# The gated chunk mixer of a two-layer block: its group stages reordered, and its input weights kept as a bf16 copy in DRAM

## Chip, cores and metric

The kernel runs on all 8 cores of one Trainium2 chip. Each core computes one of the eight batch elements; the cores exchange nothing. The time is device microseconds of the slowest core.

## What is computed

Two layers over a sequence of 2048 tokens plus 256 context tokens, with 1024 features. Layer 0 mixes tokens by a gated MLP over chunks of 128 tokens, layer 1 by window attention; each is followed by a mixture of 16 experts that every token passes through densely. The change touches only the mixer of layer 0:

```python
def chunk_gmlp(h, w_in, g_v, w_s, b_s, w_out):      # h: normalized, modulated x
    uv = jax.nn.gelu(h @ w_in)                      # w_in 1024 x 4096
    u, v = jnp.split(uv, 2, axis=-1)                # 2048 + 2048 features
    v = rmsnorm(v, g_v).reshape(bsz, n // CHUNK, CHUNK, A_GROUPS, A_GW)
    v = jnp.einsum('gpq,bcqgd->bcpgd', w_s, v) + b_s.T[None, None, :, :, None]
    return (u * v.reshape(bsz, n, A_WIDTH)) @ w_out
...
x = x + g1 * chunk_gmlp(h, ...)                     # then the experts, attention, experts
```

## The kernel before

The program is a list of operations per engine, each in the order in which it is written. `Prog.op` gives every operation its waits from the buffers that it reads and writes; an engine takes its list strictly in order, and so do the two queues that issue transfers: POOL (all transfers that cast float32 to bf16) and SP (all others). A transfer that must wait holds up everything behind it in its queue. Phases follow one another with a barrier: modulation vectors, mixer (`phase_gmlp`), experts, attention, experts, final norm.

In `phase_gmlp` the 18 token tiles of 128 are taken in five groups, four of 4 tiles and a last one of 2. All 18 tiles of x live in SBUF in float32 (`C.x_sb`). Each group goes through four stages, one group after the other:

- **A**: SP loads the x tiles of the group (L576; 512 KB each; no buffer is reused, so nothing holds these loads back). `norm_stats` (L429 to L436) clears a sum on DVE, squares each tile on ACT with an accumulated sum, takes the square root on ACT and the reciprocal on DVE. Then for each tile DVE scales it (L448), TensorE transposes eight blocks (L475) into one PSUM bank, and ACT (L482, even tiles) or DVE (L486, odd tiles) writes the modulated result to `hTg`, of which there is one buffer.
- **B**: for four column pieces of w_in (1024 x 512, read as float32 from DRAM, 2 MB, and cast to 1 MB of bf16 in flight) POOL issues the load into one of two `wi` buffers (L585). TensorE does 32 matmuls on each (L593), and ACT applies gelu to give `uT`.
- **C**: the four pieces of the v half likewise (L601, matmuls L608, gelu to `vraw`); then the squares of v for its norm on ACT (L619), their sum (L622), root (L624) and reciprocal (L626).
- **D**: for each tile DVE scales v (L631), TensorE mixes the chunk (32 small matmuls, L639 and L642), DVE multiplies by `uT` (L645), TensorE multiplies by w_out (32 matmuls, L652), and DVE scales by the gate (L655) and adds to x (L658).

So the order on every engine is A, B, C, D of group 0, then A of group 1, and so on, and every group loads all eight pieces of w_in again: 40 loads on the POOL queue. With two `wi` buffers, piece p+2 can be loaded only once the matmuls of piece p are done. At the start of the phase POOL issues the small constants, then the two halves of w_out (L561), which wait for each other because they are noted as writes of one buffer, and then pieces 0 and 1; SP issues two gate vectors and all x tiles.

Of the kernel before, what the change touches and what calls it, by code (L numbers as in the profile page):

```python
# [6 lines left out]
BF16 = mybir.dt.bfloat16  # L7
# [233 lines left out]
def build_program(stop_after=None, dbg=False):  # L241
# [94 lines left out]
    if stop_after == "A":  # L336
        return finish(C)
    phase_gmlp(C)
    if stop_after == "B":
        return finish(C)  # L340
# [166 lines left out]
def phase_gmlp(C):  # L507
    nc, P, I = C.nc, C.P, C.I
# [3 lines left out]
    wi = [R.t("wi%d" % i, [128, 8, 512], BF16) for i in range(2)]  # L512
    wiB = P.bufs("wi", 2)
# [46 lines left out]
    for h in range(2):  # L560
        P.op("pool", lambda e, h=h: e.dma_start(out=w_out[:, h * 8:(h + 1) * 8, :],  # L561
                                               in_=I.a_w_out[h * 1024:(h + 1) * 1024, :].rearrange("(c p) f -> p c f", p=128)),
             writes=[woB], dma=True)

    groups = [[0, 1, 2, 3], [4, 5, 6, 7], [8, 9, 10, 11], [12, 13, 14, 15], [16, 17]]
    ring = [1, 2, 3]
    rk = 0
    pmk = 0
    wk = 0
    tk = 0  # L570
    for g in groups:
        n = len(g)
        N = 128 * n
        for i, t in enumerate(g):
            src = I.ctx[t * 128:(t + 1) * 128, :] if t < 2 else I.x[(t - 2) * 128:(t - 1) * 128, :]
            P.op("sp", lambda e, t=t, src=src: e.dma_start(out=C.x_sb[:, t, :], in_=src), writes=[C.xB[t]], dma=True)  # L576
        norm_stats(C, g, ssall, ssBt, rstd, rstdB, [sts[0]["xn"], sts[1]["xn"]], [sts[0]["xnB"], sts[1]["xnB"]], eps, epsB)
        for i, t in enumerate(g):
            who = 1 if t < 2 else 0
            norm_transpose_tile(C, R, C.x_sb[:, t, :], C.xB[t], layer, 0, who, hTg, hTgB, i * 128, sts, 0,  # L580
                                rstd_ap=rstd[:, i:i + 1], rstdB=rstdB)
        for jj in range(4):
            s = wk % 2
            wk += 1
            P.op("pool", lambda e, jj=jj, s=s: e.dma_start(  # L585
                out=wi[s][:], in_=I.a_w_in[jj].rearrange("(c p) f -> p c f", p=128)),
                writes=[wiB[s]], dma=True)
            for j4 in range(4):
                j = jj * 4 + j4
                pb = ring[rk % 3]  # L590
                rk += 1
                for k in range(8):
                    P.op("pe", lambda e, s=s, j4=j4, k=k, pb=pb, N=N: e.matmul(  # L593
                        C.ps[pb][:, 0:N], wi[s][:, k, j4 * 128:(j4 + 1) * 128], hTg[:, k, 0:N], start=(k == 0), stop=(k == 7)),
                        reads=[wiB[s], hTgB], writes=[C.psB[pb]])
                P.op("act", lambda e, j=j, pb=pb, N=N: e.activation(out=uT[:, j, 0:N], in_=C.ps[pb][:, 0:N], func=AF.Gelu_apprx_tanh),
                     reads=[C.psB[pb]], writes=[uTB])
        for sv in range(4):
            s = wk % 2
            wk += 1  # L600
            P.op("pool", lambda e, sv=sv, s=s: e.dma_start(  # L601
                out=wi[s][:], in_=I.a_w_in[4 + sv].rearrange("(c p) f -> p c f", p=128)),
                writes=[wiB[s]], dma=True)
            for i, t in enumerate(g):
                pb = ring[rk % 3]
                rk += 1
                for k in range(8):
                    P.op("pe", lambda e, s=s, k=k, pb=pb, i=i: e.matmul(  # L608
                        C.ps[pb][:, :], hTg[:, k, i * 128:(i + 1) * 128], wi[s][:, k, :], start=(k == 0), stop=(k == 7)),
                        reads=[wiB[s], hTgB], writes=[C.psB[pb]])  # L610
                P.op("act", lambda e, sv=sv, pb=pb, i=i: e.activation(out=vraw4[:, i, sv * 512:(sv + 1) * 512], in_=C.ps[pb][:, :],
                                                                      func=AF.Gelu_apprx_tanh),
                     reads=[C.psB[pb]], writes=[vrawB4[i]])
        for i in range(n):
            P.op("dve", lambda e, i=i: e.memset(ssv[:, i, :], 0.0), writes=[ssvBt[i]])
        for i in range(n):
            for hf in range(2):
                jb = sts[(2 * i + hf) % 2]
                P.op("act", lambda e, i=i, hf=hf, jb=jb: e.activation(out=jb["xn"][:, 0:1024], in_=vraw4[:, i, hf * 1024:(hf + 1) * 1024],  # L619
                                                                    func=AF.Square, accum_out=ssv[:, i, hf:hf + 1]),  # L620
                     reads=[vrawB4[i], ssvBt[i]], writes=[ssvBt[i], jb["xnB"]])
        P.op("dve", lambda e, n=n: e.tensor_tensor(out=rstdv[:, 0:n], in0=ssv[:, 0:n, 0], in1=ssv[:, 0:n, 1], op=ALU.add),  # L622
             reads=list(ssvBt[:n]), writes=[rstdvB])
        P.op("act", lambda e, n=n: e.activation(out=rstdv[:, 0:n], in_=rstdv[:, 0:n], func=AF.Sqrt, scale=1.0 / 2048, bias=eps[:, 0:1]),  # L624
             reads=[rstdvB, epsB], writes=[rstdvB])
        P.op("dve", lambda e, n=n: e.reciprocal(out=rstdv[:, 0:n], in_=rstdv[:, 0:n]), reads=[rstdvB], writes=[rstdvB])  # L626
        for i, t in enumerate(g):
            who = 1 if t < 2 else 0
            pp = tk % 2
            tk += 1  # L630
            P.op("dve", lambda e, i=i: e.scalar_tensor_tensor(out=vraw4[:, i, :], in0=vraw4[:, i, :], scalar=rstdv[:, i:i + 1], in1=gv[:],  # L631
                                                             op0=ALU.mult, op1=ALU.mult),
                 reads=[vrawB4[i], rstdvB, gvB], writes=[vrawB4[i]])
            for b4 in range(4):
                pm = 4 + (pmk % 2)
                pmk += 1
                for jq in range(4):
                    j = b4 * 4 + jq
                    P.op("pe", lambda e, pm=pm, jq=jq, j=j, i=i: e.matmul(  # L639
                        C.ps[pm][:, jq * 128:(jq + 1) * 128], vraw4[:, i, j * 128:(j + 1) * 128], wsT[:, j // 2, :], start=True, stop=False),  # L640
                        reads=[vrawB4[i], wsB], writes=[C.psB[pm]])
                    P.op("pe", lambda e, pm=pm, jq=jq, j=j: e.matmul(  # L642
                        C.ps[pm][:, jq * 128:(jq + 1) * 128], ones1[0:1, :], bsrow[0:1, j // 2, :], start=False, stop=True),
                        reads=[bsB], writes=[C.psB[pm]])
                P.op("dve", lambda e, pm=pm, b4=b4, i=i, pp=pp: e.tensor_tensor(  # L645
                    out=prodT[pp][:, 4 * b4:4 * b4 + 4, :], in0=C.ps[pm][:, :].rearrange("p (a n) -> p a n", a=4),
                    in1=uT[:, 4 * b4:4 * b4 + 4, i * 128:(i + 1) * 128], op=ALU.mult),
                    reads=[C.psB[pm], uTB], writes=[prodB[pp]])
            for half in range(2):
                pb = 6 + half  # L650
                for j in range(16):
                    P.op("pe", lambda e, pb=pb, j=j, half=half, pp=pp: e.matmul(  # L652
                        C.ps[pb][:, :], prodT[pp][:, j, :], w_out[:, j, half * 512:(half + 1) * 512], start=(j == 0), stop=(j == 15)),
                        reads=[prodB[pp], woB], writes=[C.psB[pb]])
                P.op("dve", lambda e, pb=pb, half=half, who=who, pp=pp: e.tensor_tensor(  # L655
                    out=tmpf[pp][:, half * 512:(half + 1) * 512], in0=C.ps[pb][:, :], in1=C.gbc[:, who, half * 512:(half + 1) * 512], op=ALU.mult),
                    reads=[C.psB[pb], C.gbcB[who]], writes=[tmpfB[pp]])
            P.op("dve", lambda e, t=t, pp=pp: e.tensor_tensor(out=C.x_sb[:, t, :], in0=C.x_sb[:, t, :], in1=tmpf[pp][:], op=ALU.add),  # L658
                 reads=[tmpfB[pp], C.xB[t]], writes=[C.xB[t]])


def _const_tables():
# [526 lines left out]
```

How the kernel before makes its waits and increments, by code:

```python
        def run(ename, eng):  # L152
            waited = {}
            for o in self.ops[ename]:
                need = {}
                for d in o.deps:
                    if d.sem is None:
                        continue
                    key = d.sem
                    if need.get(key, (0,))[0] < d.cnt:
                        need[key] = (d.cnt, d.sem)
                for key, (cnt, sem) in need.items():
                    if waited.get(key, 0) >= cnt:
                        continue
                    eng.wait_ge(sem, cnt)
                    waited[key] = cnt
                inst = o.fn(eng)
                if o.dma:
                    inst.then_inc(o.sem, 16)
                elif o.need_inc:
                    inst.then_inc(o.sem, 1)
```

## Time and profile before

| | us |
|---|---|
| median of 2 runs | 5187.08 (5054.29 and 5319.87) |
| profiled execution | 5052.77 |
| its span, slowest core (core 0) | 5051.2 |
| spans of the eight cores | 5020.7 to 5051.2 |
| TensorE matmuls busy in the span | 3964.6 (78%) |
| PE idle in the mixer until a w_in load landed | 53.1 + 49.9 |

The mixer with its first loads takes the stretch from about 230 to 1214 us of the span. The rows further down are of core 0, the slowest. A row of the timeline gives the start, the length, the engine and line, what is written from what, how many instructions were merged, and in brackets the idle time before it with what ended that. A row of the windows gives for a stretch the busy time and the number of instructions of each engine, then the granted TensorE clock as a share of 2.4 GHz, the share in which the 16 DMA engines were busy, and GB/s written.

### The profile page before, as it was taken

To read this page: it belongs to the slowest core of one execution; us is meant where nothing else is said; L and a number is where in the kernel's file an instruction comes from. 1 tells how busy PE (TensorE), PEld (TensorE's weight loads), DVE (VectorE), ACT (ScalarE), POOL (GpSimd) and SP (SyncE) were. 2 spreads that over 40 slices of the span, in tenths; PEclk is the share of its full clock that TensorE was granted. 3 is DMA by queue.
4 is the path that set the end of the run, shared out by engine and by line. 5 is a ranking of instruction groups with operands and counts; after the bars stand their busy time and mean duration, and the time that the engine had idled before them with its cause. 6 is when DMAs were issued, how large, how long until landed. Compare 5 with 4: busy or idle time off the path is not lost.

```text
span 5051.2 us, 56891 instructions; the slowest of 8 cores (5020.7 to 5051.2 us)
## 1 busy us (share of the span) xinstructions
PE 3964.6 (78%) x19632; PEld 1843.6 (36%) x19632; DVE 1704.1 (34%) x2756; ACT 928.8 (18%) x1703; POOL 1509.0 (30%) x897
## 2 busy tenths in 40 slices
PE   3255667564599999999999566666399999999994
PEld 0022222231244454454444332332244444444442
DVE  0002122122344444444443453111344444444444
ACT  0021211313211111111111323444311111111112
POOL 1000000000044444444454301222044444444442
PEclk7576777776699999999999798888599999999997
DMA  9681422415012113113111021000212121212111
GB/s 142 92 157 17 67 32 35 67 25 84 1 26 42 34 26 51 26 26 51 26 26 26 26 20 25 1 1 8 47 26 45 31 46 30 47 29 47 30 26 71
DMA packets 191273, 206.31 MB, mean 41 GB/s; under 512 B 33544, under 2 KB 165768, under 8 KB 190728
## 3 DMA queue, kind: packets, MB, share of 16 engines
q0 software_dynamic: 167424, 178.63, 23.4%
q1 hardware_dynamic: 23568, 24.03, 1.6%
q8 instruction: 164, 2.69, 0.2%
q14 instruction: 117, 0.96, 0.1%
HBM read 372.78 MB, written 8.49 MB: 75 GB/s over the span
## 4 chain that ended last, share of the span: by engine, by line
PE 71%; DMA 9%; DVE 6%; ACT 6%; issue 5%; POOL 4%; DVEq 0%; ACTq 0%; POOLq 0%; SPq 0%
PE ps L875 19%; PE ps L871 19%; PE ps L893 15%; DMA pb_wi<-a_w_in 4%; PE ps L652 3%; POOL x_sb L901 3%; DMA pa_wa<-ada_w 2%; PE ps L593 2%; PE ps L608 2%; PE ps L1050 2%; PE ps L1159 2%; PE ps L1131 2%; DVE hT L486 1%; ACT hT L482 1%; PE ps L639 1%
## 5 line engine op out<-in xcount | busy, mean ns | idle before, releaser
L901 POOL TENSOR_TENSOR x_sb<-x_sb,pc_tmpf 128x1024 f32<-128x1024 f32 x544 | 1260.9, 2352 | 1746.7 <-DVE pc_tmpf L897 1746.7
L871 PE MATMUL ps<-hT,pc_wg 128*128 128x512 bf16 (+1 forms) x4608 | 1037.2, 368 | 0.0
L875 PE MATMUL ps<-hT,pc_wu 128*128 128x512 bf16 (+1 forms) x4608 | 1034.3, 367 | 1.7 <-DVE pc_A L880 1.7
L893 PE MATMUL ps<-pc_wd,pc_A 128*128 128x512 bf16 x4352 | 964.3, 379 | 13.9 <-DVE pc_tmpf L897 13.9
L897 DVE SCALAR_TENSOR_TENSOR pc_tmpf<-ps,sm_gatesv,gbc 128x512 f32<-128x512 f32 x1088 | 815.9, 750 | 342.0 <-POOL x_sb L901 160.0
L880 DVE TENSOR_TENSOR pc_A<-ps,pc_sg 128x512 bf16<-128x512 f32 x576 | 380.9, 661 | 1293.7 <-PE ps L871 835.4
L878 ACT ACTIVATE pc_sg<-ps 128x512 bf16<-128x512 f32 x576 | 330.4, 574 | 2478.4 <-PE ps L871 2169.1
L871 PEld LDWEIGHTS ps<-hT,pc_wg 128*128 128x128 bf16 x4608 | 451.4, 98 | 493.9 <-issue 3.3
L875 PEld LDWEIGHTS ps<-hT,pc_wu 128*128 128x128 bf16 x4608 | 450.8, 98 | 492.2 <-issue 4.2
L893 PEld LDWEIGHTS ps<-pc_wd,pc_A 128*128 128x128 bf16 x4352 | 417.3, 98 | 539.2 <-issue 59.0
L585 POOL DMA_DIRECT2D pb_wi<-a_w_in x20 | 17.6, 879 | 665.1 <-PE ps L593 592.9
L1167 ACT ACTIVATE pd_PT<-ps 128x512 bf16<-128x512 f32 x312 | 162.4, 604 | 216.2 <-PE ps L1159 211.9
L593 PE MATMUL ps<-pb_hTg,pb_wi 128*128 128x512 bf16 (+1 forms) x640 | 147.0, 398 | 69.7 <-DMA pb_wi<-a_w_in 53.1
L639 PE MATMUL ps<-pb_wsT,pb_vraw 128*128 128x128 bf16 x288 | 81.5, 283 | 128.9 <-DVE pb_vraw L631 128.9
L608 PE MATMUL ps<-pb_wi,pb_hTg 128*128 128x512 bf16 x576 | 141.8, 409 | 50.0 <-DMA pb_wi<-a_w_in 49.9
L652 PE MATMUL ps<-pb_wout,pb_prodT 128*128 128x512 bf16 x576 | 162.8, 452 | 18.3 <-DVE pb_prodT L645 18.3
L390 PE MATMUL ps<-pa_wa,pa_sclhs 128*2 128x512 bf16 x192 | 78.2, 583 | 124.7 <-DMA pa_wa<-ada_w 90.1
L1159 PE MATMUL ps<-pd3b_qz,pd_kT 128*128 128x512 bf16 x312 | 103.7, 436 | 80.0 <-POOL pd3b_qz L1155 80.0
L622 DVE TENSOR_TENSOR pb_rstdv<-pb_ssv 128x4 f32<-128x4 f32 (+1 forms) x5 | 0.8, 162 | 433.6 <-ACT pb_xn L619 433.6
L475 PE MATMUL ps<-sm_ident_b,pb_xn 128*128 128x128 bf16 x144 | 18.2, 307 | 149.6 <-DVE pb_xn L448 107.2
L432 ACT ACTIVATE pb_xn<-x_sb 128x1024 bf16<-128x1024 f32 x18 | 18.8, 1047 | 594.6 <-DVE pb_ssall L429 348.9
L1172 PE MATMUL ps<-pd_v,pd_PT 128*128 128x65 bf16 x1248 | 86.7, 200 | 51.1 <-ACT pd_PT L1167 49.7
(149 smaller groups left out, 2134.2 us busy)
## 6 DMA issues: line engine op xcount, KB each, us to landing
pb_wi<-a_w_in POOLq DMA_DIRECT2D x40, 1024.0 KB, 10.3
pc_wg<-moe_w_gate POOLq DMA_DIRECT2D x32, 1024.0 KB, 9.5
pc_wu<-moe_w_up POOLq DMA_DIRECT2D x32, 1024.0 KB, 13.8
pc_wd<-moe_w_down POOLq DMA_DIRECT2D x32, 1024.0 KB, 18.1
pa_wa<-ada_w POOLq DMA_DIRECT2D x24, 1024.0 KB, 16.0
x_sb<-x SPq DMA_DIRECT2D x16, 512.0 KB, 29.8
out<-pf_ob SPq DMA_DIRECT2D x16, 512.0 KB, 2.6
pb_wout<-a_w_out POOLq DMA_DIRECT2D x2, 2048.0 KB, 34.0
```

The lines of the kernel that those rows point to most:

```text
L593: P.op("pe", lambda e, s=s, j4=j4, k=k, pb=pb, N=N: e.matmul(C.ps[pb][:, 0:N], wi[s][:, k, j4 * 128:(j4 + 1) * 128], hTg[:, k, 0:N], start ...
L608: P.op("pe", lambda e, s=s, k=k, pb=pb, i=i: e.matmul(C.ps[pb][:, :], hTg[:, k, i * 128:(i + 1) * 128], wi[s][:, k, :], start=(k == 0), st ...
L652: P.op("pe", lambda e, pb=pb, j=j, half=half, pp=pp: e.matmul(C.ps[pb][:, :], prodT[pp][:, j, :], w_out[:, j, half * 512:(half + 1) * 512] ...
L871: P.op("pe", lambda en, k=k, f=f, pg=pg: en.matmul(C.ps[pg][:, 0:N], Wg[s][:, k, f * 128:(f + 1) * 128], C.hT[:, k, tok0:tok0 + N], start= ...
L875: P.op("pe", lambda en, k=k, f=f, pu=pu: en.matmul(C.ps[pu][:, 0:N], Wu[s][:, k, f * 128:(f + 1) * 128], C.hT[:, k, tok0:tok0 + N], start= ...
L878: P.op("act", lambda en, q=q, pg=pg: en.activation(out=sg[q][:, 0:N], in_=C.ps[pg][:, 0:N], func=AF.Silu), reads=[C.psB[pg]], writes=[sgB[q]])
L880: P.op("dve", lambda en, f=f, q=q, pu=pu: en.tensor_tensor(out=A[:, f, tok0:tok0 + N], in0=C.ps[pu][:, 0:N], in1=sg[q][:, 0:N], op=ALU.mul ...
L893: P.op("pe", lambda en, f=f, half=half, pb=pb, t=t: en.matmul(C.ps[pb][:, :], A[:, f, t * 128:(t + 1) * 128], Wd[s][:, f, half * 512:(half ...
L897: P.op("dve", lambda en, half=half, pb=pb, t=t, who=who, q=q: en.scalar_tensor_tensor(out=tmpf[q][:, half * 512:(half + 1) * 512], in0=C.p ...
L901: P.op("pool", lambda en, t=t, q=q: en.tensor_tensor(out=C.x_sb[:, t, :], in0=C.x_sb[:, t, :], in1=tmpf[q][:], op=ALU.add), reads=[tmpfB[q ...
L1159: P.op("pe", lambda e, bi=bi, kc=kc, hk=hk, pq=pq, mi=mi: e.matmul(C.ps[bi][:, :], kT[:, hk, kc:kc + 128], qz[pq][:].rearrange("p a b -> p ...
L1167: P.op("act", lambda e, bi=bi, pq=pq: e.activation(out=PT[pq][:, bi, :], in_=C.ps[bi][:, :], func=AF.Exp, scale=0.125), reads=[C.psB[bi]], ...
```

## The change

Stage A becomes a function of its own, stages B and C another, D a third. They are issued as A(0), then for every group BC(g), A(g+1), D(g). So the norm and the transposes of the next group stand, on every engine and queue, ahead of stage D of this group. The x loads of a group are in its stage A, on the SP queue.

The pieces of w_in are loaded by `load_piece`. In group 0 each is loaded as before on the POOL queue, and SP then stores the bf16 tile to a new DRAM tensor `wsc`, with 8 KB contiguous for each partition. In groups 1 to 4 SP loads the piece from `wsc`, and POOL issues nothing. The store reads the `wi` buffer, so piece p+2 of group 0 waits for it too.

```diff
--- before.py
+++ after.py
@@ -568,7 +568,21 @@
     pmk = 0
     wk = 0
     tk = 0
-    for g in groups:
+    st8 = {"rk": 0, "pmk": 0, "wk": 0, "tk": 0}
+    wsc = nc.dram_tensor("w_in_bf16", [8, 128, 8 * 512], BF16, kind="Internal").ap()
+    wscB = P.bufs("wsc", 8)
+
+    def load_piece(pc, s, gi):
+        if gi == 0:
+            P.op("pool", lambda e: e.dma_start(out=wi[s][:], in_=I.a_w_in[pc].rearrange("(c p) f -> p c f", p=128)),
+                 writes=[wiB[s]], dma=True)
+            P.op("sp", lambda e: e.dma_start(out=wsc[pc], in_=wi[s][:].rearrange("p c f -> p (c f)")),
+                 reads=[wiB[s]], writes=[wscB[pc]], dma=True)
+        else:
+            P.op("sp", lambda e: e.dma_start(out=wi[s][:].rearrange("p c f -> p (c f)"), in_=wsc[pc]),
+                 reads=[wscB[pc]], writes=[wiB[s]], dma=True)
+
+    def stage_a(g):
         n = len(g)
         N = 128 * n
         for i, t in enumerate(g):
@@ -579,12 +593,15 @@
             who = 1 if t < 2 else 0
             norm_transpose_tile(C, R, C.x_sb[:, t, :], C.xB[t], layer, 0, who, hTg, hTgB, i * 128, sts, 0,
                                 rstd_ap=rstd[:, i:i + 1], rstdB=rstdB)
+
+    def stage_bc(g, gi):
+        n = len(g)
+        N = 128 * n
+        rk, wk = st8["rk"], st8["wk"]
         for jj in range(4):
             s = wk % 2
             wk += 1
-            P.op("pool", lambda e, jj=jj, s=s: e.dma_start(
-                out=wi[s][:], in_=I.a_w_in[jj].rearrange("(c p) f -> p c f", p=128)),
-                writes=[wiB[s]], dma=True)
+            load_piece(jj, s, gi)
             for j4 in range(4):
                 j = jj * 4 + j4
                 pb = ring[rk % 3]
@@ -598,9 +615,7 @@
         for sv in range(4):
             s = wk % 2
             wk += 1
-            P.op("pool", lambda e, sv=sv, s=s: e.dma_start(
-                out=wi[s][:], in_=I.a_w_in[4 + sv].rearrange("(c p) f -> p c f", p=128)),
-                writes=[wiB[s]], dma=True)
+            load_piece(4 + sv, s, gi)
             for i, t in enumerate(g):
                 pb = ring[rk % 3]
                 rk += 1
@@ -624,6 +639,11 @@
         P.op("act", lambda e, n=n: e.activation(out=rstdv[:, 0:n], in_=rstdv[:, 0:n], func=AF.Sqrt, scale=1.0 / 2048, bias=eps[:, 0:1]),
              reads=[rstdvB, epsB], writes=[rstdvB])
         P.op("dve", lambda e, n=n: e.reciprocal(out=rstdv[:, 0:n], in_=rstdv[:, 0:n]), reads=[rstdvB], writes=[rstdvB])
+        st8["rk"], st8["wk"] = rk, wk
+
+    def stage_d(g):
+        n = len(g)
+        pmk, tk = st8["pmk"], st8["tk"]
         for i, t in enumerate(g):
             who = 1 if t < 2 else 0
             pp = tk % 2
@@ -657,6 +677,16 @@
                     reads=[C.psB[pb], C.gbcB[who]], writes=[tmpfB[pp]])
             P.op("dve", lambda e, t=t, pp=pp: e.tensor_tensor(out=C.x_sb[:, t, :], in0=C.x_sb[:, t, :], in1=tmpf[pp][:], op=ALU.add),
                  reads=[tmpfB[pp], C.xB[t]], writes=[C.xB[t]])
+
+
+        st8["pmk"], st8["tk"] = pmk, tk
+
+    stage_a(groups[0])
+    for gi, g in enumerate(groups):
+        stage_bc(g, gi)
+        if gi + 1 < len(groups):
+            stage_a(groups[gi + 1])
+        stage_d(g)
 
 
 def _const_tables():
```

## Rows read from the trace of the kernel before

**Rows 1.** Windows by stage of core 0: busy us (and count) per engine, clock, DMA share, GB/s.

```profile
core 0: us, PE busy (x) PEld busy (x) DVE busy (x) ACT busy (x) POOL busy (x), PEclk, DMA share, GB/s
...
230.00:306.00 76.00, 4.05 (x32) 3.10 (x32) 8.98 (x30) 13.50 (x26) 4.72 (x6) 0.50 1.02 222
306.20:383.30 77.10, 64.14 (x256) 26.72 (x256) 0.00 (x0) 19.80 (x32) 6.12 (x7) 0.88 0.69 97
383.30:398.10 14.80, 0.00 (x0) 0.01 (x1) 2.69 (x3) 10.93 (x19) 0.87 (x1) 0.58 0.70 109
398.10:479.70 81.60, 63.67 (x256) 26.82 (x256) 26.37 (x29) 0.00 (x0) 0.00 (x0) 0.70 0.00 0
479.70:510.00 30.30, 4.05 (x32) 3.10 (x32) 10.38 (x31) 11.89 (x25) 0.00 (x0) 0.58 0.00 0
510.10:586.00 75.90, 61.05 (x256) 25.68 (x256) 0.00 (x0) 19.80 (x32) 6.11 (x7) 0.92 0.68 97
714.10:786.60 72.50, 62.20 (x256) 26.11 (x256) 0.00 (x0) 19.80 (x32) 6.12 (x7) 0.91 0.68 97
913.20:989.60 76.40, 64.42 (x256) 26.49 (x256) 0.00 (x0) 19.79 (x32) 6.11 (x7) 0.88 0.68 96
1103.30:1166.00 62.70, 36.88 (x192) 21.10 (x192) 0.00 (x0) 11.61 (x24) 5.25 (x6) 0.76 0.73 101
```

**Rows 2.** Waits of PE between 300 and 1240 us: total us, times, longest.

```profile
PE ps L593 <- DMA pb_wi<-a_w_in: 53.1, 6, 27.4
PE ps L608 <- DMA pb_wi<-a_w_in: 49.9, 17, 9.0
```

**Rows 3.** Timeline of PE, the first pieces of group 0.

```profile
306.22 16.14 PE L593 MATMUL ps<-pb_hTg,pb_wi 128*128 128x512 bf16 x64 [27.43 <-DMA pb_wi<-a_w_in]
327.39 15.66 PE L593 MATMUL ps<-pb_hTg,pb_wi 128*128 128x512 bf16 x64 [5.03 <-DMA pb_wi<-a_w_in]
```

**Rows 4.** Timeline of POOL, the loads of pieces 2 and 3 of group 0.

```profile
316.01 0.87 POOL L585 DMA_DIRECT2D pb_wi<-a_w_in  x1 [41.76 <-PE ps L593]
322.90 0.87 POOL L585 DMA_DIRECT2D pb_wi<-a_w_in  x1 [6.02 <-PE ps L593]
```

**Rows 5.** Transfers issued, from the page: count, KB each, median us to landing.

```profile
pb_wi<-a_w_in POOLq DMA_DIRECT2D x40, 1024.0 KB, 10.3
...
x_sb<-x SPq DMA_DIRECT2D x16, 512.0 KB, 29.8
out<-pf_ob SPq DMA_DIRECT2D x16, 512.0 KB, 2.6
```

**Rows 6.** Timeline of the SP queue in the attention phase, two 1 MB loads.

```profile
2841.67 0.33 SPq L985 DMA_DIRECT2D pd_cosT<-rope  x1
2846.66 0.33 SPq L986 DMA_DIRECT2D pd_sinT<-rope  x1
```

**Rows 7.** Waits of the SP queue around those loads.

```profile
SPq L165 <- DMA pd_sinT<-rope: 6.2, 1, 6.2
SPq L165 <- DMA pd_cosT<-rope: 4.6, 1, 4.6
```

**Rows 8.** Windows with dense matmuls in the expert phase.

```profile
2000.00:2100.00 100.00, 100.00 (x496) 48.26 (x495) 41.06 (x58) 12.28 (x22) 48.05 (x25) 1.00 0.24 36
```

**Rows 9.** Windows at the start of the phase, and while a piece is loaded alone.

```profile
260.00:272.00 12.00, 2.02 (x16) 1.55 (x16) 4.88 (x12) 3.66 (x8) 0.66 (x1) 0.50 1.04 278
...
321.00:333.00 12.00, 6.97 (x26) 2.62 (x24) 0.00 (x0) 1.74 (x4) 0.87 (x1) 0.86 1.11 162
```

**Rows 10.** Tile of w_out until 310 us: its two loads and their landing times.

```profile
L561 POOL DMA_DIRECT2D pb_wout<-a_w_out x2: 926/1000/1073, 231.3 to 271.3; - x2
...
DMA to landing us min/median/max: 28.5/34.0/39.4
```

**Rows 11.** Tile of wi until 312 us: landing times of pieces 0 and 1.

```profile
DMA to landing us min/median/max: 33.6/35.6/37.7
```

**Rows 12.** Timeline between stage C and stage D of group 0.

```profile
395.23 0.18 DVE L626 RECIPROCAL pb_rstdv<-pb_rstdv 128x4 f32<-128x4 f32 x1 [1.84 <-ACT pb_rstdv L624]
```

**Rows 13.** Timeline of stage A of group 1, between D(0) and B(1).

```profile
481.99 1.06 ACT L432 ACTIVATE pb_xn<-x_sb 128x1024 bf16<-128x1024 f32 x1 [86.93 <-DVE pb_ssall L429]
...
487.93 1.01 PE L475 MATMUL ps<-sm_ident_b,pb_xn 128*128 128x128 bf16 x8 [8.26 <-DVE pb_xn L448]
...
507.77 2.14 DVE L486 TENSOR_SCALAR pb_hTg<-ps,sm_cols 128x128 bf16<-128x128 bf16 x5 [0.46 <-DVE pb_hTg L486]
```

## Prediction

> **What bounds the kernel now.** I read the windows by stage first. Outside the mixer nothing is touched, so the question is how much of the stretch from 230 to 1214 us is not matmul at full speed. In the expert phase TensorE is busy all of a 100 us window at a granted clock of 1.00, that is 2.4 GHz [rows 8]. In the mixer the stages with eight weight pieces (B and C, "BC" below) take 77.1, 75.9, 72.5, 76.4 and 62.7 us [rows 1]. What they would take without waiting comes from the POOL queue: it issues a load when a buffer comes free, and the buffers of pieces 0 and 1 came free at 316.01 and 322.90 [rows 4]. So 32 matmuls of 512 columns take 6.9 us at 2.4 GHz (0.215 us each), and eight pieces 55.2 us. BC of a full group is 17 to 22 us longer.
>
> Where these go is in the waits and in TensorE's timeline: pieces go in pairs, 64 matmuls and then some 3 to 5 us until a w_in load lands [rows 2, 3]. The pause costs twice. The first pair after it takes 15.66 us where 13.8 would do [rows 3]: after idling, the engine runs at 1.2 GHz before it is granted 2.4 again, hence a mean clock of 0.88 to 0.92 in BC [rows 1]. The load is the limit: issued at 316.01, its piece's matmuls begin at 327.39, 11.4 us later, of which 10.3 us is landing [rows 3, 4, 5]. One buffer's load (11.4) and the other buffer's piece (6.9 and up) don't fit in two pieces of matmuls (13.8). Three further stretches matter: 76 us of loads ahead of the first piece [rows 1], 14.8 us between C and D and 30.3 us between D and the next B [rows 1].
>
> **Term 1, the pieces of groups 1 to 3.** A load from the copy is 1 MB without a cast, 8 KB for each partition. The trace has that very transfer: the cosine table, 1 MB of 128 rows of 8 KB, issued on SP in 0.33 us, kept the queue waiting 4.6 us until it landed; the next one, which shared the engines with two other transfers, 6.2 us [rows 6, 7]. I take 5.0 us from a free buffer to data, bounds 4.9 and 11.4 (as now). As 5.0 is under 6.9, no piece waits. BC is then 55.2 us, plus 0.4 for the last matmul's end and 0.4 for a slow start: 56.0. Today B starts after transposes at a clock of 0.50 to 0.58 [rows 1]; after the change it comes straight behind D's dense matmuls. Gains: 75.9, 72.5 and 76.4 less 56.0 each, together 56.8.
>
> A rule of the Trainium skill speaks against this: the page "TensorE: Matmul & The Clock Gate", Part 1, says that a die goes to 13/16 of the clock once three of its cores run dense matmuls. This case's trace disagrees, for all eight cores run the expert phase and the slowest core is granted 1.00 there [rows 8]. By the page BC would be 68 us instead of 56.
>
> **Term 2, group 4.** Two tiles, so a piece is half as long, 3.45 us, and now the load of 5.0 doesn't fit: a pair of pieces takes 5.4 + 3.45 = 8.9 us (0.4 for waking both engines). Three such pairs and a last pair of 6.9 are 33.6 us; with 1.5 us at the low clock 35. Today 62.7: gain 27.7. Bounds: 20 if the pauses keep the clock at 0.76, as there now [rows 1], and 29.
>
> **Term 3, the start.** Today 18 x tiles (9 MB) share the DMA engines with w_out: 278 GB/s in all [rows 9], and the two halves of w_out, one behind the other, land 39.4 and 28.5 us after issue at 231.3 and 271.3 [rows 10]. Pieces 0 and 1 are issued at 272.4 and land 33.6 and 37.7 us later, at 306.0 and 311 [rows 11]. In the new order SP issues only four x tiles before it meets the first store, and the other 14 tiles (7.2 MB) go elsewhere. Data up to the first half's landing: gate vectors 1 MB, x 2 MB, constants 0.8, half of w_out 2 = 5.8 MB at the stretch's mean of 222 GB/s [rows 1] from 230 on: 256, and some us later for a start slower than the mean: 259. The second half: a lone cast load of 1 MB lands in 10.3 us [rows 5], of which the bytes take 6.2 at 162 GB/s [rows 9], so 4 us go before and after; 2 MB at 278 GB/s are 7.5 us, at 200 they are 10: 272. Piece 0 follows directly with 6.2 us and the same 4: 282. hTg is ready about then too: TensorE's last transposes ended 27.4 us before 306.2 [rows 3], at 279, and their evacuation takes 3 or 4. With both ends so near each other I take B(0) to start at 286, a gain of 20. Bounds: 5, if the other traffic only filled gaps, and 24.
>
> **Term 4, the stores of group 0.** Eight stores of 1 MB on SP, each behind the landing of its piece. A 512 KB store lands in 2.6 us [rows 5]; for 1 MB I take 4.5. It starts with the piece's matmuls (6.9 us), so the buffer is not held longer. But it shares the DMA engines with the cast load of the next piece, and group 0 is still bound by those loads. Moving it takes 2.7 us at most of another load's time. Half of the stores fall into the 5 us between an issue and its first bytes: four that cost up to 2.7, less what the idle pause absorbs: 6 us lost, bounds 0 and 20. The page "DMA: Bandwidth & Descriptors", Anatomy of one DMA, warns that the receipt of a write can be surprisingly long when the target is HBM; the 2.6 us of the output stores don't show it. Were a store 10 us long, each pair would lose some 5, in all the 20 of the bound.
>
> **Term 5, the boundaries.** Stage A(g+1) moves in front of D(g). Today, from the end of C to D is 14.8 us and from the end of D to B 30.3, together 45.1 [rows 1]. New: the reciprocal of v's norm ends at 395.4, 12.1 after C's end [rows 12]; the squares of x can start then. From the first square to the last evacuation today is 481.99 to 509.9, 27.9 us [rows 13]. Then comes DVE's scaling of v with 2.6 us (395.4 to 398.1 [rows 12, 1]) and D begins: 12.1 + 27.9 + 2.6 = 42.6. After D, TensorE goes straight on with B. Gain 2.4 per boundary, four of them: 9, bounds 0 and 14. So the reordering hides almost nothing: the work of A sits in front of D on ACT, DVE and TensorE alike, and D waits in its place; what is hidden is only the tail of D on DVE (L655, L658).
>
> **What else moves.** Of stage A four more operations change their queue position: the x loads. In SP they stand behind store 7 of group 0, which waits for the landing of piece 7, some 7 us before C ends. Four tiles (2 MB at 222 GB/s, 9.5 us, plus the store) land about 6 us after C's end, and ACT asks for the first at 12.1: hidden by 6 us. In later groups they stand behind the load of piece 7, issued when piece 5 is done, 14 us before C's end: hidden. Pieces 0 and 1 of the next group stand behind them but have the 82 us of D [rows 1]. Lines on POOL vanish; nothing waited for POOL but these loads.
>
> **Sum.** -56.8 - 27.7 - 20 + 6 - 9 = -107.5 against the profiled 5052.77 us (its span is 5051.2), so 4945; I write 4947, as a core with shorter pauses today, and so less to gain, may then be the last. The other run shown is 5319.87 and the median 5187; the sum is against the lower of the two, with which the profiled execution agrees.
>
> **Rivals.**
> (a) **The loads are slower than the table's**, because eight cores read at once for long: landing 8 us instead of 4.6. For it: sinT's 6.2. Against it: cosT was read by all cores too. Each pair of pieces then waits about 1.5 us and gets the slow start of 1.9 again: 3 pauses of 3.4 us in 3 groups, and 13 us in group 4 (4 pairs, 3.2 each), together 44 less gain: 4991.
> (b) **The clock is held at 13/16 in BC.** 12 us more in four groups, less what group 0 hides: about 44 (36, and 8 in group 4): 4991. Against it [rows 8].
> (c) **The x loads become the wait.** If they land in 29.8 us, as the median now [rows 5], instead of about 13, issued 7 us before C ends: 23 after, 11 later than ACT asks, in group 0, and 4 in the others: 20 us: 4967. Against it: now 18 are in flight together.
> (d) **Slower than before.** The mechanism is the piece load from the copy alone: if it takes longer than the cast, all of groups 1 to 4 pay. Terms 3 to 5 give 23 us; each us of landing over today's 10.3 costs 3 per full group and 4 in the last, 13; it decides above 12 us. At the 29.8 us of the x loads, 19.5 x 13 - 23 = 230 more: 5283. Only [rows 5] speaks for it, and [rows 6, 7] against.
> (e) **The copy isn't what the loads take**, or they aren't shortened: only terms 3 to 5: 5030.
>
> **Chances.** Forecast 0.70, with its own range 4922 to 4972; (a) 0.10, (b) 0.05, (c) 0.07, (d) 0.03, (e) 0.05. 2% is about what a measurement can tell here, and it lies at 4952, inside the forecast's range: some 0.66 of the forecast's 0.70 falls below, and none of the others. So faster 0.47, within 2% 0.50, slower 0.03. The range holds the forecast, (a), (b) and (c): 4915 to 5000.
>
> **What would show it.** Right: no wait for a w_in load in BC of groups 1 to 3, BC of 56 us at a clock near 1.00; landing near 5 us on SP; the first piece at about 286; C to D about 43 us, D to B none. Wrong: pauses between pieces, a wait for x in stage A, BC(0) over 90 us, or D no longer 82 us.

## The result

The changed kernel is faster, by about 2%: the ratio of its runs to those of the kernel before is 0.9804, 95% interval 0.9753 to 0.9855. So it is clear that it is faster, and not whether by more than 2%. Its profiled execution took 4951.95 us against 5052.77, and was forecast at 4947. Some executions of either kernel had a lower TensorE clock on one die or both and are left out of the comparison (all but one of 4999.34 us; the other six in it took 4942.14 to 4951.95), and they are why the plain medians (4999.34 of 11 runs, 5309.07 of 10 before) are higher.

### The profile page after: what moved, and what is told of

Same layout as the page of the kernel before. It is cut to its first block, busy times and chain, and to the rows that moved or that the text cites. A ratio compares the mean times of both kernels' runs of the same rounds, so it can differ in the third digit from the quotient of the medians.

```text
span 4950.3 us, 56912 instructions; the slowest of 8 cores (4935.4 to 4950.3 us)
## 1 busy us (share of the span) xinstructions
PE 3945.8 (80%) x19632; PEld 1842.4 (37%) x19632; DVE 1703.9 (34%) x2756; ACT 928.6 (19%) x1703; POOL 1481.2 (30%) x865
## 4 chain that ended last, share of the span: by engine, by line
PE 73%; DMA 6%; DVE 6%; ACT 6%; issue 5%; POOL 4%; DVEq 0%; ACTq 0%; POOLq 0%; SPq 0%
PE ps L905 19%; PE ps L901 19%; PE ps L923 15%; PE ps L672 3%; POOL x_sb L931 3%; DMA pa_wa<-ada_w 2%; PE ps L623 2%; PE ps L610 2%; PE ps L1189 2%; PE ps L1080 2%; PE ps L1161 2%; DVE hT L486 1%; ACT hT L482 1%; DMA pb_wi<-a_w_in 1%; PE ps L659 1%
## 5 line engine op out<-in xcount | busy, mean ns | idle before, releaser
L610 PE MATMUL ps<-pb_hTg,pb_wi 128*128 128x512 bf16 (+1 forms) x640 | 132.8, 371 | 16.5 <-DMA pb_wi<-a_w_in 13.6
L623 PE MATMUL ps<-pb_wi,pb_hTg 128*128 128x512 bf16 x576 | 130.6, 388 | 18.1 <-DMA pb_wi<-a_w_in 13.6
L839 PE MATMUL ps<-pc_wr,hT 128*128 128x16 bf16 x272 | 12.3, 174 | 142.1 <-ACT hT L482 77.8
L482 ACT ACTIVATE hT<-ps,sm_cols 128x128 bf16<-128x128 bf16 x208 | 95.2, 458 | 145.8 <-PE ps L475 128.5
## 6 DMA issues: line engine op xcount, KB each, us to landing
pb_wi<-a_w_in POOLq DMA_DIRECT2D x8, 1024.0 KB, 13.9
```

The lines of the kernel that those rows point to most:

```text
L610: P.op("pe", lambda e, s=s, j4=j4, k=k, pb=pb, N=N: e.matmul(C.ps[pb][:, 0:N], wi[s][:, k, j4 * 128:(j4 + 1) * 128], hTg[:, k, 0:N], start ...
L623: P.op("pe", lambda e, s=s, k=k, pb=pb, i=i: e.matmul(C.ps[pb][:, :], hTg[:, k, i * 128:(i + 1) * 128], wi[s][:, k, :], start=(k == 0), st ...
```

## The profile after

The windows by stage of the changed kernel, core 6, its slowest (columns as in [rows 1]): BC of group 0, C to D, D, BC of group 1, C to D, D, and BC of groups 2, 3 and 4.

```profile
287.90:371.80 83.90, 66.14 (x256) 26.81 (x256) 0.00 (x0) 19.80 (x32) 5.26 (x6) 0.82 0.92 193
371.80:414.20 42.40, 4.12 (x34) 3.17 (x33) 11.04 (x28) 22.80 (x44) 0.00 (x0) 0.54 0.25 82
414.20:496.40 82.20, 64.33 (x256) 27.05 (x257) 26.38 (x29) 0.00 (x0) 0.00 (x0) 0.68 0.00 1
496.40:551.90 55.50, 55.46 (x257) 24.95 (x255) 1.96 (x6) 19.79 (x32) 0.00 (x0) 1.00 0.48 163
551.90:594.20 42.30, 4.23 (x33) 3.20 (x33) 11.05 (x28) 22.80 (x44) 0.00 (x0) 0.55 0.11 35
594.20:676.40 82.20, 64.33 (x256) 27.05 (x256) 26.37 (x29) 0.00 (x0) 0.00 (x0) 0.69 0.00 1
676.40:732.40 56.00, 55.58 (x257) 24.90 (x255) 1.95 (x6) 19.80 (x32) 0.00 (x0) 1.00 0.48 164
857.40:912.70 55.30, 55.30 (x258) 24.95 (x255) 1.95 (x6) 19.80 (x32) 0.00 (x0) 1.00 0.42 152
1024.50:1061.80 37.30, 30.33 (x193) 18.94 (x191) 1.94 (x4) 11.61 (x24) 0.00 (x0) 0.95 0.47 170
```

Against [rows 1], BC of groups 1 to 3 fell from 75.9, 72.5 and 76.4 us to 55.5, 56.0 and 55.3, with TensorE busy throughout and the clock up from about 0.9 to 1.00; group 4 fell from 62.7 to 37.3. Two stretches grew: BC of group 0 from 77.1 to 83.9, and C to D from 14.8 to 42.4. For the latter, the 30.3 us between D and the next B are gone: D ends at 496.4 and BC(1) begins at 496.4.

Each figure so far is that of one core, the slowest of its kernel. Over the eight cores of the two profiled executions they are these (us):

| | before | after |
|---|---|---|
| BC of groups 1 to 3 | 69.9 to 77.9 | 55.4 to 56.3 |
| BC of group 4 | 57.4 to 62.6 | 35.0 to 38.0 |
| BC of group 0 | 70.3 to 78.0 | 80.6 to 88.3 |

PE's waits for the weights in the whole mixer, which answer to [rows 2] (total us, times, longest):

```profile
PE ps L610 <- DMA pb_wi<-a_w_in: 13.6, 3, 9.4
PE ps L623 <- DMA pb_wi<-a_w_in: 13.6, 3, 6.7
PE ps L623 <- DMA pb_wi<-w_in_bf: 2.9, 3, 1.8
PE ps L610 <- DMA pb_wi<-w_in_bf: 2.6, 1, 2.6
```

Of 103.0 us, 27.2 are left for the cast loads of group 0 and 5.5 for all 32 loads from the copy. The first of them in the timeline of PE (answers to [rows 3]), the issues on POOL (to [rows 4]), and the landing times of pieces 0 and 1 (to [rows 11]):

```profile
287.92 16.71 PE L610 MATMUL ps<-pb_hTg,pb_wi 128*128 128x512 bf16 x64 [9.45 <-DMA pb_wi<-a_w_in]
308.55 9.74 PE L610 MATMUL ps<-pb_hTg,pb_wi 128*128 128x512 bf16 x32 [3.92 <-DMA pb_wi<-a_w_in]
...
496.45 27.79 PE L610 MATMUL ps<-pb_hTg,pb_wi 128*128 128x512 bf16 x128
524.07 27.79 PE L623 MATMUL ps<-pb_wi,pb_hTg 128*128 128x512 bf16 x128
```

```profile
262.95 0.88 POOL L561 DMA_DIRECT2D pb_wout<-a_w_out  x1 [31.01 <-DMA pb_wout<-a_w_out]
263.82 1.76 POOL L577 DMA_DIRECT2D pb_wi<-a_w_in  x2
298.29 0.88 POOL L577 DMA_DIRECT2D pb_wi<-a_w_in  x1 [32.70 <-PE ps L610]
```

```profile
DMA to landing us min/median/max: 23.9/27.2/30.5
```

The first piece starts at 287.9 instead of 306.2. Both parts of the way there got shorter: the first half of w_out holds POOL for 31.0 us and not 39.1, so pieces 0 and 1 are issued at 263.8 and not 272.4, and piece 0 then lands in 23.9 us and not 33.6. In group 1 there is no bracket at all: 128 matmuls of the u half and 128 of the v half in 27.79 us each. The transfers (answers to [rows 5]):

```profile
pb_wi<-w_in_bf SPq DMA_DIRECT2D x32, 1024.0 KB, 5.0
...
x_sb<-x SPq DMA_DIRECT2D x16, 512.0 KB, 9.2
pb_wi<-a_w_in POOLq DMA_DIRECT2D x8, 1024.0 KB, 13.9
w_in_bf<-pb_wi SPq DMA_DIRECT2D x8, 1024.0 KB, 8.0
```

A piece from the copy lands in 5.0 us instead of 10.3; the cast loads left in group 0 take 13.9, beside stores that take 8.0.

Lastly the timeline between C and D of group 0, the whole of the new wait in order (compare [rows 12, 13]):

```profile
383.79 0.18 DVE L641 RECIPROCAL pb_rstdv<-pb_rstdv 128x4 f32<-128x4 f32 x1 [1.84 <-ACT pb_rstdv L639]
...
384.08 1.06 ACT L432 ACTIVATE pb_xn<-x_sb 128x1024 bf16<-128x1024 f32 x1 [0.46 <-DVE pb_ssall L429]
...
411.57 2.34 DVE L651 SCALAR_TENSOR_TENSOR pb_vraw<-pb_vraw,pb_rstdv,pb_gv 128x2048 bf16<-128x2048 bf16 x1
```

v's norm is ready at 384.0, but the scaling of v that D needs (L651) comes 27.6 us later in DVE's order, behind all of stage A of the next group.

## The experiments

Theory: the gain is the pauses between pieces (85 of some 107 us), then the start (20), and the order of the stages gives about 9. Rival: the new order, which lets stage A of one group run before stage D of the one before, carries a large part. Where no interval is given, there were too few times for one, and the times stand themselves.

**The order alone.**

```diff
 def load_piece(pc, s, gi):
-    if gi == 0:
+    if True:
         P.op("pool", ... in_=I.a_w_in[pc] ...)
-        P.op("sp", ... out=wsc[pc] ...)
-    else: ...
```

> The new order of the stages alone; every group loads its pieces with the cast from a_w_in on the POOL queue, as before, and nothing is stored. My theory (term 5: stage A stands in front of D on ACT, DVE and TensorE, so only D's tail on DVE is hidden): four boundaries of 42.6 instead of 45.1 us, total about 5043 us against 5052.8, a ratio of 0.998; pauses between the pieces as before, first piece at 306 us since all x loads are issued at once again (nothing on SP waits). Rival (the overlap of the groups carries a large part of the gain): 20 us or more less, under 5030.

Measured: ratio 0.9979 (0.9956 to 1.0003), profiled execution 5027.68. PE's timeline for BC(1) of this kernel:

```profile
505.86 13.98 PE L605 MATMUL ps<-pb_hTg,pb_wi 128*128 128x512 bf16 x64
523.50 15.66 PE L605 MATMUL ps<-pb_hTg,pb_wi 128*128 128x512 bf16 x64 [3.67 <-DMA pb_wi<-a_w_in]
543.16 16.56 PE L618 MATMUL ps<-pb_wi,pb_hTg 128*128 128x512 bf16 x64 [4.00 <-DMA pb_wi<-a_w_in]
```

The pauses are as before; only the first pair, straight behind D, runs in 13.98 us at full clock. The profiled execution is 25 us below the kernel before and would by itself have met the rival's "under 5030"; but the five times in the comparison go from 5027.68 to 5055.87, and their mean is 11 us below that of the kernel before. So the new order by itself can't be told from no change, and the large part that the rival gives it is not there.

**The copy alone.**

```diff
 for gi, g in enumerate(groups):
     stage_bc(g, gi)
+    stage_d(g)
     if gi + 1 < len(groups):
         stage_a(groups[gi + 1])
-    stage_d(g)
```

> The bf16 copy in DRAM alone, with the stages in the old order A, B, C, D of one group after the other. My theory: the whole gain but the 10 us of the boundaries and the better start of B: about 4962 us, BC of groups 1 to 3 at 56 to 58 us (the slow clock at its start is back, about 2 us each), 14.8 us from C to D and 30.3 from D to B. Rival (the overlap carries a large part): 4990 or more.

Measured: ratio 0.9833 (0.9791 to 0.9876), profiled execution 4969.8, another 4963.0. The windows of BC of groups 1 and 4 on core 5:

```profile
499.00:557.40 58.40, 58.16 (x256) 25.43 (x256) 0.00 (x0) 19.79 (x32) 0.00 (x0) 0.95 0.47 152
...
1039.00:1082.20 43.20, 35.15 (x192) 21.36 (x192) 0.00 (x0) 11.61 (x24) 0.00 (x0) 0.83 0.41 146
```

As expected, 2 to 3 us more per full group, which start after transposes at the low clock. In group 4 this core takes 6 more, but the eight cores take 35.9 to 43.2, on the mean 2 more than those of the changed kernel. Of the 101 us of gain, 83 are there without the new order. The 18 that the order adds on top of the copy are some 11 at the four boundaries, which term 5 priced, and most of the rest a B that starts at full clock, which the prediction counted in term 1.

**The x loads ahead.**

```diff
 def stage_a(g):
-    for i, t in enumerate(g): ... dma_start(out=C.x_sb[:, t, :], in_=src)
...
+for g in groups:
+    for i, t in enumerate(g): ... dma_start(out=C.x_sb[:, t, :], in_=src)
 stage_a(groups[0])
```

> The changed kernel, but SP issues the loads of all 18 x tiles before the first group, as the kernel before did. My theory (term 3: the 14 other tiles share the DMA engines with w_out and pieces 0 and 1): the first piece starts at about 306 us again instead of 288, total about 4969 us, 18 to 20 more than the changed kernel. Rival (the start came earlier for another reason, as the x loads only fill gaps): first piece at 288, 4950.

Measured: 4967.38 and 4975.53, ratio 0.9843 (0.9801 to 0.9886). PE's timeline:

```profile
305.70 15.31 PE L607 MATMUL ps<-pb_hTg,pb_wi 128*128 128x512 bf16 x64 [27.04 <-DMA pb_wi<-a_w_in]
```

The first piece is back at 305.7, and the profiled execution is 15 us longer. So the earlier start is a side effect of the stores: SP meets one and stops issuing x loads, which no longer share the DMA engines with w_out. The two kernels above fit: with the order alone, where nothing is stored, the first piece starts at 303.6 on the slowest core, and with the copy alone, in the old order, at 288.4.

**Three buffers instead of the copy.**

```diff
-wi = [R.t("wi%d" % i, [128, 8, 512], BF16) for i in range(2)]
+wi = [R.t("wi%d" % i, [128, 8, 512], BF16) for i in range(3)]
...
-s = wk % 2
+s = wk % 3
```

> The kernel before with three wi buffers instead of two (gv and half of the bias row moved elsewhere in SBUF to make room), no copy, old order, all 40 cast loads on POOL. Theory A (the pause comes from 11.4 us from free buffer to data with only two buffers, while the bytes of a cast piece move in 6.2 us, under the 6.9 of its matmuls): pauses vanish in groups 1 to 3 without any copy, BC 56 to 59 us there, about 60 in group 0 and 50 in group 4 (bound by 6.2 us per piece); total about 4970. Rival B (the cast load itself is too slow, about 10 us per piece whatever the buffers): BC stays at 70 or more, total above 5030.

Measured: 4980.3, expected about 4970. PE's timeline of BC(1), core 7:

```profile
507.16 29.69 PE L594 MATMUL ps<-pb_hTg,pb_wi 128*128 128x512 bf16 x128 [4.25 <-DVE pb_ssv L616]
536.68 27.79 PE L609 MATMUL ps<-pb_wi,pb_hTg 128*128 128x512 bf16 x128
```

The old cast loads still land in 10.4 us, and no pause is left in the full groups. Theory A holds: what cost was the time from a free buffer to data with two buffers, not the rate of the loads. By the slowest core a third buffer alone gives 72 of the 101 us. That core and its neighbour, 7 and 6, were granted a clock of 0.81 in group 0 (see the last section) and took 68.6 and 66.2 us there, where the other six took 57.1 to 58.1. These six ended at 4951.5 to 4963.8, and the cores of the copy alone at 4951.7 to 4968.3: either remedy is worth about the same. The third buffer is ahead in group 0, where nothing is stored beside the loads (57 to 58 us against 81 to 87), the copy in group 4 (35.9 to 43.2 against 44.6 to 47.2) and at the start.

**Twice the stores.**

```diff
 P.op("sp", ... dma_start(out=wsc[pc], in_=wi[s] ...), reads=[wiB[s]], ...)
+P.op("sp", ... dma_start(out=wsc2[pc], in_=wi[s] ...), reads=[wiB[s]], ...)
```

> The changed kernel, but SP stores every piece of group 0 twice, the second time to a DRAM tensor that nothing reads. The cost of the stores is doubled. My theory (term 4: a store takes DMA time from the cast load beside it, 6 us for eight stores; BC of group 0 measured 83.9 us against 77.1 before): with the second store still running when the matmuls of its piece are done, the buffer is held too, so 8 to 20 us more, BC(0) at 92 to 104 us, total about 4965. Rival (the stores cost nothing and BC(0) is longer for its more frequent pauses alone): BC(0) stays at 84, total 4950.

Measured: 4970.64. BC(0) on core 6:

```profile
290.80:392.50 101.70, 67.14 (x250) 27.21 (x254) 0.00 (x0) 19.79 (x32) 5.25 (x6) 0.80 0.99 235
```

17.8 us longer than with one store, with the DMA engines busy 0.99 of the time. Doubling adds more than the first store did (6.8). With two, POOL also waits for a store before it may load (28.5 us in three waits), which it never does with one. The stores do cost, and term 4 was of the right kind.

**The copy through the other queue.**

```diff
 else:
-    P.op("sp", lambda e: e.dma_start(out=wi[s][:]..., in_=wsc[pc]), ...)
+    P.op("pool", lambda e: e.dma_start(out=wi[s][:]..., in_=wsc[pc]), ...)
```

> The changed kernel, but groups 1 to 4 load the bf16 copy through the POOL queue instead of SP: same bytes, same 8 KB rows, no cast, another issuer. It tells the two differences between the old and the new load apart. Theory A (the gain is in the bytes and the row length: 2.7 us of engine time instead of 6.2): landing about 6.5 us (2 us more to start than on SP), 7.5 from free to data, so pauses of 0.5 to 1 us per pair, BC 58 to 60, total about 4965. Theory B (the gain is the issuer: POOL takes 4 us or more to start whatever the transfer): landing 8 us or more, pauses of 2 us per pair with a slow clock after some of them, BC 62 to 66, total 4975 to 4990.

Measured: ratio 0.9806 (0.9785 to 0.9826), times of 4952.9 to 4958.9, expected 4965. The transfers and PE's timeline of BC(1) on core 5:

```profile
pb_wi<-w_in_bf POOLq DMA_DIRECT2D x32, 1024.0 KB, 6.0
```

```profile
495.08 13.98 PE L610 MATMUL ps<-pb_hTg,pb_wi 128*128 128x512 bf16 x64
510.06 13.97 PE L610 MATMUL ps<-pb_hTg,pb_wi 128*128 128x512 bf16 x64 [1.00 <-DMA pb_wi<-w_in_bf]
523.92 20.95 PE L623 MATMUL ps<-pb_wi,pb_hTg 128*128 128x512 bf16 x96
```

Theory A: landing is 1 us longer than on SP, where the cast load took 5 more. The pauses that theory A expected are there on this core (BC(1) takes 57.4 us), but on most cores at the full clock it takes 55.4. So the load got short by what it moves, hardly by its issuer. Whether by the missing cast, the halved bytes or the longer rows was not tried.

**Stage A inside D.** Where the new order failed, in DVE's and ACT's lists, a different one should work. Both this edit and the next are given in outline, not as code.

```diff
 def stage_d(g, nxt):
     for i, t in enumerate(g):
         scale v (DVE)
+        if i == 0: squares and root of the next x tiles (ACT)
         for b4 in range(4): mix (PE), products (DVE)
+        if i == 0: reciprocal (DVE)
+        scale x tile i of the next group (DVE)
         for half in range(2):
+            if half == 1: 8 transposes (PE), 8 evacuations (ACT) of it
             w_out matmuls (PE), gate (DVE)
         add to x (DVE)
```

> The changed kernel with stage A(g+1) not ahead of D(g) but inside it: squares and root of x on ACT while D's first tile runs, and for each tile of D one tile of the next group scaled on DVE after the products, its eight transposes between the two halves of the w_out matmuls, its evacuation on ACT alone. My theory (term 5: what costs is that A stands in front of D, 42.4 us of idle TensorE per boundary, of which 27.9 are A's): C to D falls back to 15 us, D grows by 1 to 2 us per tile (0.9 of transposes, 0.75 on DVE), so 20 to 24 us less at each of four boundaries, total about 4860. Rival (A must stand before D, or its pieces only move the wait into D, whose tiles wait for DVE): under 30 us gained in all, above 4920.

Measured: 4869.94 and 4871.08. The windows of C to D, D and BC(1), core 3:

```profile
370.50:385.40 14.90, 0.02 (x2) 0.03 (x1) 2.69 (x3) 14.01 (x26) 0.00 (x0) 0.57 0.61 203
385.40:469.60 84.20, 66.31 (x288) 28.75 (x288) 29.19 (x34) 15.19 (x35) 0.00 (x0) 0.69 0.00 0
470.70:526.20 55.50, 55.41 (x256) 24.97 (x256) 1.20 (x9) 19.81 (x32) 0.00 (x0) 1.00 0.48 170
```

C to D is 14.9 us again instead of 42.4, and D is only 2 us longer with all of A in it. That is the overlap that the order of the changed kernel does not reach: 82 us more, where it saved 2.7 us at each of four boundaries. The expected 4860 was 10 us too low.

**And v scaled early.**

```diff
         for b4 in range(4): mix (PE), products (DVE)
+        scale v of tile i + 1 (DVE)
...
         w_out matmuls (PE), gate (DVE), add to x (DVE)
```

> As the kernel with A inside D, and DVE scales v of the next tile right after the products of this one, ahead of the gate and the add on x, so that TensorE needn't wait at the start of a tile. Theory: the wait of 4.6 us at the start of 13 of the 18 tiles goes (95 us of it in all of the mixer now, of which the first tile of each group stays), and with it the slow clock after it, about 6 us per tile: 80 us less than with A inside D alone, total about 4785. Rival (DVE itself is full in D: 2.35 + 2.8 + 1.4 + 1.2 + 0.75 = 8.5 us of 20 per tile says no, but the scaling delays the gate of the first half and so the banks): under 30 us.

Measured: ratio 0.9528 (0.9473 to 0.9583), times of 4799.3, 4803.36 and 4845.15. PE's waits, and the window of D(0), core 5:

```profile
PE ps L690 <- DVE pb_vraw L666: 69.3, 5, 14.9
```

```profile
386.90:454.40 67.50, 61.97 (x288) 28.31 (x288) 28.92 (x34) 15.08 (x34) 0.00 (x0) 0.76 0.00 0
```

18 waits for the scaled v have become 5, and D takes 67.5 us instead of 84.2. The profiled execution is 67 us shorter, of the expected 80.

**Three buffers as well.**

```diff
-wi = [... for i in range(2)]
+wi = [... for i in range(3)]
```

> The kernel with A inside D and the early scaling of v, and three wi buffers beside the copy. It tells what is left of the piece loads once both remedies are there. Theory: groups 1 to 3 have no pauses already, so nothing there; group 0 (two buffers, cast loads of 6.2 us of bytes plus 2.7 of store) falls from about 84 us to 68 to 72 (with three buffers and no stores it took 69), group 4 from 36 to 32: 15 to 20 us less, about 4783. Rival (group 0 is held by the DMA engines' time, not by the buffers, as 8.9 us of transport per piece are more than 6.9 of matmuls): group 0 at 78 or more, total 4795.

Measured: ratio 0.9464 (0.9387 to 0.9541), times of 4786.77, 4789.62 and 4795.61. PE's timeline in group 0, core 7:

```profile
286.97 8.80 PE L611 MATMUL ps<-pb_hTg,pb_wi 128*128 128x512 bf16 x32 [13.63 <-DMA pb_wi<-a_w_in]
298.17 7.07 PE L611 MATMUL ps<-pb_hTg,pb_wi 128*128 128x512 bf16 x32 [2.40 <-DMA pb_wi<-a_w_in]
307.76 8.65 PE L611 MATMUL ps<-pb_hTg,pb_wi 128*128 128x512 bf16 x32 [2.53 <-DMA pb_wi<-a_w_in]
...
348.82 16.96 PE L624 MATMUL ps<-pb_wi,pb_hTg 128*128 128x512 bf16 x64 [1.73 <-DMA pb_wi<-a_w_in]
```

BC(0) lasts from 287.0 to 365.8, 78.8 us, and 75.6 to 80.9 over the cores: my theory (68 to 72) falls, and the rival is the nearer. The 69 us "with three buffers and no stores" that it started from was the core at the lower clock; the others took 57 to 58. So with three buffers the stores cost group 0 about 20 us: with one beside each load, the pieces come at intervals of 10 us. By the times alone the extra buffer isn't shown to gain, as its interval overlaps that of the two-buffer version. The stages show that it does: BC(4) takes 28.3 to 29.0 us on every core, and 36.9 to 40.8 with two buffers. Both versions beat both kernels. Three buffers without the copy, and with A inside D, were not tried.

**w_out late.**

```diff
 def load_piece(pc, s, gi):
     if gi == 0:
         ...
+        if pc == 7: the two loads of w_out (POOL)
```

> As the kernel with three buffers and the copy, but the two loads of w_out are issued behind the load of the last piece of group 0 instead of ahead of the first. Theory (term 3 goes on: ahead of the first piece stand the 4 MB of w_out, 31 and some 14 us one behind the other): pieces 0 to 2 land by 260, the first matmul waits for hTg alone and starts at 279 to 282 instead of 288, 6 to 8 us less; w_out's 22 to 26 us fit between the last piece's issue and D(0), total about 4775. Rival: w_out lands after D(0) asks for it, the wait only moves: no gain or a loss of up to 15.

The profiled execution took 5141.37 us, with a granted clock of 0.81 on core 0 in the B and C of most groups and in the first expert phase, so its total is no answer. The stages are. PE's waits and its timeline, core 0:

```profile
PE ps L713 <- DMA pb_wout<-a_w_out: 13.0, 1, 13.0
```

```profile
279.32 35.36 PE L612 MATMUL ps<-pb_hTg,pb_wi 128*128 128x512 bf16 x128 [3.90 <-DVE pb_ssv L632]
```

The first piece does start at 279.3 with no wait for a load, but D(0) then waits 13.0 us for w_out. In another run the four cores of the die that was granted the full clock took 4774.5 to 4784.8 us, and in the kernel before this one those of the same die 4768.9 to 4781.6: no gain, the wait moved, as the rival had it.

## Why the prediction was right and where it was not

**The step that failed is the last, from the time to the chances.** The text called 2% "about what a measurement can tell here", and from that gave "within 2%" a chance of 0.50 and faster 0.47. Its own forecast of 4947 was a gain of 106 us, a ratio of 0.979. What the runs showed instead: the interval reaches 0.5% to either side, so that 1 lies nearly four such half-widths away; no time of the kernel before in the comparison is under 5050, and six of seven after are at 4942 to 4952. No row stood behind the 2%. The sum was trusted to some 25 us in its range and then not in its verdict. That the measured ratio came out on the line of 2% itself is chance, and speaks for neither side.

The mechanism was right, and so was the size of most terms. By the slowest cores:

- **Term 1** (groups 1 to 3, 56.8 us): 58.0. The twin transfer of [rows 6, 7], 4.6 us, foretold the landing of 5.0 within half a microsecond, and the clock of 1.00 behind D is there.
- **Term 2** (group 4, 27.7): 25.4. The pair of pieces takes what was summed, with pauses of 0.6 to 2.7 us; 2 us were missed on waits for ACT and restarts.
- **Term 3** (start, 20): 18.3, and its cause is shown by the kernel with the x loads ahead. The start at 286 was in part luck. The sum had the second half of w_out land at 272 and piece 0 at 282; they landed at 280.9 and 287.7, and the 4 us that the text added on top, for the nearness of hTg, hid most of it. (The 6.2 us for the bytes of a piece at 162 GB/s are 6.5 for its 1024 KB.)
- **Term 4** (stores, 6 lost): 6.8 lost, but its parts were mis-sized. A store took 8.0 us and not 4.5. That did not show, since no wait of POOL in group 0 ended with a store; what cost is the cast load beside it, 13.9 us where it took 10.3.
- **Term 5** (boundaries, 2.4 each): C to D 42.4 and D to B 0, against 45.1: 2.7 each. The fourth boundary, where stage A has only two tiles, is shorter (31.6 before, 28.8 after) and gains the same. That the order of the stages hides almost nothing was the central claim, and the kernel with the order alone bears it out (0.9979), as the one with A inside D shows what hiding it is worth.
- **The sum.** These give 106 us; the spans differ by 100.9. SP issues the first load of the expert phase at 1113.4 us instead of 1216.2, 102.8 earlier. The five stages D of core 6 took together some 4 us more than those of core 0 before, and some 2 us are lost behind the mixer; no term foresaw either.
- **The slowest core is not the mean core.** The sum started from core 0, the slowest before, and allowed 2 us for that. Over all eight cores the mean gains are 55.3 (term 1), 23.6 (term 2) and 16.9 (term 3), the stores cost 9.0, and the mean span fell by 97 us and not 107. Terms 2, 3 and 4 are each some 3 to 4 us too kind by that.
- **Rivals.** The x loads were asked for at 384.1 and had been issued from 365.0 on with 9.2 us to land: hidden, rival (c) falls. Rival (a) falls with the landing of 5.0, (d) and (e) with the profile. Rival (b) is not in the profile of the changed kernel, where BC is at 1.00, but it does happen, at its price of 12 us for each BC of a full group: the last section has it.
- **The range** of 4915 to 5000 holds the profiled execution, which lies 5 us from the forecast; its upper part was there for rivals that did not come.

## What to carry over

With two buffers, compare the time from a free buffer to landed data with the compute time of one piece, not the transfer's rate with it; a third buffer or a shorter transfer cures the same pause, and here either was worth about the same. Moving a stage ahead of another in program order hides it only if the engines whose lists it enters have room there: here it had to go inside D, tile by tile, and not in front. An extra wait on an issue queue has effects far from it: here it held back loads and brought the start forward by 18 us. And before a gain is called too small to tell, it has to be set against the scatter of the times, not against a round figure.

## What the runs showed of the hardware

**A third level of the clock, and it comes in pairs of cores.** Dense matmuls ran at a granted clock of 1.00 on all eight cores in the expert phases of the two profiled kernels (for the one before see [rows 8]). But other executions show 0.81 for long stretches. The kernel with the copy on POOL, cores 1 and 2, which are on the same die, in two windows of its expert phases:

```profile
2000.00:2100.00 100.00, 100.00 (x497) 48.30 (x495) 41.09 (x58) 12.29 (x22) 44.25 (x21) 1.00 0.30 44
4500.00:4600.00 100.00, 100.00 (x383) 41.42 (x381) 34.75 (x48) 9.56 (x16) 38.73 (x19) 0.81 0.21 32
```

```profile
2000.00:2100.00 100.00, 100.00 (x414) 44.92 (x413) 37.71 (x53) 9.30 (x17) 44.24 (x21) 0.81 0.11 17
4500.00:4600.00 100.00, 97.71 (x450) 43.12 (x449) 44.31 (x61) 10.68 (x18) 54.80 (x26) 1.00 0.20 32
```

In the first window core 2 gets 414 matmuls done where core 1 does 497, and in the second it is the other way round. Core 0 is granted what core 1 is, and core 3 what core 2 is; the four cores of the other die are granted 1.00 in both windows. TensorE was busy at least 97% of either window on all four cores of this die, at the lower clock or not. The kernel with w_out late shows the same pairs: cores 0, 1, 4 and 5 have 0.81 in the first of these windows and cores 2, 3, 6 and 7 in the second, and the others 1.00. The Trainium skill's page "TensorE: Matmul & The Clock Gate", Part 1, names this level, 13/16, as what a whole die gets once three of its cores run dense matmuls. The runs agree on the level. They do not show that a whole die gets it, nor that it must come. The prediction's sentence that the trace disagrees was right for the profile of before and too strong for the chip.

**It came in the mixer too.** BC(1) of core 2 in the kernel with the copy on POOL:

```profile
501.90:569.30 67.40, 67.40 (x257) 27.74 (x255) 1.96 (x6) 19.79 (x32) 3.71 (x7) 0.81 0.30 109
```

Cores 2 and 3 took 67.4 us for it, cores 0 and 1 took 55.4: 12 us, as rival (b) had it. In the kernel with three buffers and no copy, the pair was 6 and 7, in group 0; core 7 between 330 and 370 us:

```profile
330.00:370.00 40.00, 40.00 (x154) 16.62 (x153) 0.00 (x0) 11.38 (x20) 4.37 (x5) 0.81 0.86 126
```

Core 6 has 0.81 there too. Why a pair gets it, and why only sometimes, was not tried and stays open.
